# Gate features of block 2: the sigmoid from exponent and logarithm on ACT, in two halves a unit apart, in place of an exponential on ACT and a reciprocal on DVE

## The chip, the cores and the metric

The kernel runs as one program on one core of a Trainium2 chip. The metric is the device time of one execution in microseconds; the kernel is run several times and the median is taken. The profile is one more execution, recorded by the hardware profiler. The engines are named as the profile names them: PE is TensorE, PEld its weight loads, DVE VectorE, ACT ScalarE, POOL GpSimd, SP the queue that issues most DMAs.

## The reference, cut to what matters

Two blocks of two layers each, on 256 tokens of 1024 features. Block 2 has 256 more tokens, the context, beside them in its first layer. What the change touches is how block 2 gates the outputs of its two mixers. The gates' inputs are columns of one projection `p = h @ w_in`:

```python
# layer 0 of block 2 (512 rows: tokens and context)
aq, ak, av, hu, ag, hg = split_cols(p, EVEN_SPLITS)      # ag, hg: 512 columns each
y = concatenate([y_a * silu(ag), y_b * silu(hg)])        # global attention, Hyena branch
# layer 1 of block 2 (256 rows)
wq, wk, wv, nq, nk, nv, wg, ng = split_cols(p, ODD_SPLITS)
y = concatenate([y_w * silu(wg), y_n * silu(ng)])        # window, neighbourhood attention
x = x + gate * (y @ w_out)
```

`silu(x)` is `x * sigmoid(x)`. The four matrices have 8 x 128 columns in each layer, so there are 16 groups of 128 gate features.

## The kernel before, in words

The five engines run five streams written out by hand in one Python function; semaphores order them, and every engine takes its instructions strictly in the order in which they are written. Weights are fp32. Each quarter of a slab (1024 columns per partition) is split in two parts for the matmuls: ACT copies it to the rounded `w_high` (L1278), then DVE subtracts to get `w_low` (L1650). A product is three matmuls (L582, L583, L584). There are four split buffers. A split is written into ACT's and DVE's streams by `splits.due(...)`: at that place every quarter is split whose buffer has by then been used up on PE.

Block 2's attention runs over units u = 0 to 31 (`attention2`). In layer 0 a unit is one head of one tile of 128 query rows, and PE makes the scores of two units at once (L980); the scores are 512 wide for the two token tiles and 256 wide for the two context tiles. In layer 1 the first 16 units are window attention (kind W, with one small ACT exponential more, for the sink) and the last 16 neighbourhood attention (kind N), each 512 wide, scores at L1002.

In iteration u PE issues: the scores of u; the transposes of the softmax of u-1 (L1013, `second`), which wait for ACT's exponential; then the filler, which is a few steps of the projection by features (`feature_groups`, L582 to L584); then the product with the values of u-2 (L1031). One group of 128 features is 8 steps. In layer 0 there are 4 steps per unit, so a group ends every second unit (always an odd one); in layer 1 there are 2, so a group ends every fourth. Layer 0 has 20 groups: 12 go to the Hyena branch, the last 8 are gate features, ended in units 19, 21, 23, 25, 27, 29, 31 and 32. All 8 groups of layer 1 are gate features, ended in units 3, 7, ..., 31. A group is collected in one of the three PSUM banks 5 to 7; attention uses banks 0 to 4.

ACT in iteration u: copy of the transposed softmax of u-1 out of PSUM (L1285); exponential of the scores of u (L1513 in layer 0, L1314 in layer 1), which waits for DVE's maximum; `take_features` for the group that ended in u (L1494); the split that has come due; scaled copy of the output of u-2 (L1526).

DVE in iteration u: the split that has come due (`w_low` waits for ACT's `w_high`); mask and maximum of the scores of u (L2068, or L2075 and L2076), and the bias that ACT's exponential waits for; the reciprocal of the sum of u-1 (L2057, one column); `take_features` for the group that ended in u-1, which for gate features is `silu_finish`: add 1 (L2025), reciprocal (L2027), product with the feature itself (L2029). The last frees the bank.

Block 1 of the same kernel computes its own gates in the way that the change brings to block 2: |x| (L1383), exponential (L1390) and logarithm (L1392) on ACT, the exponent on DVE (L1782), the last exponential on ACT (L1398).

After the units of layer 0 DVE goes on with the hidden layers of the Hyena filter (L2150 on), then gates the attention output with `ag` (L2168). After those of layer 1 PE transposes the outputs (L1057), DVE gates them, and the last projection follows.

Of the kernel before, what the change touches and what calls it, by code (L numbers as in the profile page):

```python
# [211 lines left out]
def two_blocks(nc, A, C, out):  # L212
    ctx = ExitStack()
    with ctx:
# [250 lines left out]
        sin_ready = Signal(sem("sin_ready"), [(0,), (1,)])  # L465
        taps_guess = Signal(sem("taps_guess"), [(0,), (1,)])
        conv_begun = Signal(sem("conv_begun"), [(c,) for c in range(HY_CH)])
        silu_exp = Signal(sem("silu_exp"), [(l, c) for l in range(LAYERS) for c in range(8)])
        gates_of = [(l, n) for l in range(LAYERS) for n in range(6 * TILES)]
        gate_logged = Signal(sem("gate_logged"), gates_of)  # L470
        gates_ready = Signal(sem("gates_ready"), gates_of)
# [21 lines left out]
        def bank(*key):  # L493
            return banks[number[key][0]]
# [740 lines left out]
        def _(act):  # L1235
# [246 lines left out]
            def take_features(l, key):  # L1482

                c = key[2]
                splits.due(*key)
                if l == 0 and c < HY_CH:
                    act.wait_ge(*filled(*key))
                    run(A_(uc[:, c, :], bank(*key)[:, :], ACT.Identity, scale=conv_w[:, 1, c:c + 1], bias=conv_w[:, 3, c:c + 1]),
                        conv_begun.by(c))
                else:  # L1490
                    n, dst = (N4, (ag, hg)) if l == 0 else (SEQ, (wgT, ngT))
                    c -= HY_CH
                    act.wait_ge(*filled(*key))
                    run(A_(dst[c // 4][:, c % 4, :], bank(*key)[:, 0:n], ACT.Exp, scale=-1.0), silu_exp.by(l, c))  # L1494

            def attention2(l):
                U = units_of_block2(l)
                for u in range(len(U) + 2):
                    if 1 <= u <= len(U):
                        n = (2 if U[u - 1][0] == "G" and U[u - 1][2] >= TILES else 4) * P  # L1500
                        if u >= 3:
                            act.wait_ge(*filled("o", 2 + l, u - 3))
                        copy_out(PT[:, (u - 1) % 2, 0:n], bank("p", 2 + l, u - 1, 0)[:, 0:n], "p", 2 + l, u - 1, 0)
                    if u < len(U):
                        splits.due("s", 2 + l, u)
                        kind, h, t = U[u]
                        n = SEQ if kind == "G" and t >= TILES else N4
                        if kind == "G":

                            act.wait_ge(*bias_ready.at(2, u))  # L1510
                            if u >= 2:
                                act.wait_ge(*filled("p", 2 + l, u - 2, 0))
                            run(A_(S[:, u % 2, 0:n], bank("s", 2, u)[:, 0:n], ACT.Exp, bias=stat[:, u % 4, 1, 0:1],  # L1513
                                   scale=SCALE, accum_out=stat[:, u % 4, 2, 0:1]), emptied("s", 2, u))
                        else:
                            softmax_exp(2 + l, u, n, S[:, u % 2, 0:n], kind, SCALE)
                    for key in ended_in[(2 + l, u)]:
                        take_features(l, key)
                    if u >= 2:
                        kind, h, t = U[u - 2]  # L1520
                        dst = {"G": o2_tok, "W": o3_tok, "N": y3_tok}[kind]
                        key = ("o", 2 + l, u - 2)
                        splits.due(*key)
                        act.wait_ge(*filled(*key))
                        act.wait_ge(*sum_inverted.at(*key[1:]))
                        run(A_(dst[:, t, h * DH:(h + 1) * DH], bank(*key)[:, 0:DH], ACT.Copy, scale=stat[:, (u - 2) % 4, 2, 1:2]),  # L1526
                            emptied(*key))
# [88 lines left out]
        def _(dve):  # L1616
# [399 lines left out]
                    run(V.tensor_copy(small[:, 3:4], small[:, 3:4]), heads_ready.by(l, j))  # L2016
                run.settle()

            def silu_finish(l, key):

                c = key[2] - HY_CH
                n, dst = (N4, (ag, hg)) if l == 0 else (SEQ, (wgT, ngT))
                g = dst[c // 4][:, c % 4, :]
                dve.wait_ge(*silu_exp.at(l, c))
                run(V.tensor_scalar(g, g, 1.0, None, ALU.add))  # L2025
                run.settle()
                run(V.reciprocal(g, g))  # L2027
                run.settle()
                run(V.tensor_tensor(g, g, bank(*key)[:, 0:n], ALU.mult), emptied(*key))  # L2029

            def take_features(l, key):
                splits.due(*key)
                c = key[2]
                if l or c >= HY_CH:
                    return silu_finish(l, key)

                dve.wait_ge(*conv_begun.at(c))
                b = bank(*key)[:, :].rearrange("p (s n) -> p s n", s=2)
                u = uc[:, c, :].rearrange("p (s n) -> p s n", s=2)
                for s in range(2):  # L2040
                    run(V.scalar_tensor_tensor(out=u[:, s, 1:SEQ], in0=b[:, s, 0:SEQ - 1], scalar=conv_w[:, 0, c:c + 1],
                                               in1=u[:, s, 1:SEQ], op0=ALU.mult, op1=ALU.add))
                run.settle()
                for s in range(2):
                    run(V.scalar_tensor_tensor(out=u[:, s, 0:SEQ - 1], in0=b[:, s, 1:SEQ], scalar=conv_w[:, 2, c:c + 1],  # L2045
                                               in1=u[:, s, 0:SEQ - 1], op0=ALU.mult, op1=ALU.add), emptied(*key) if s else None)

            def attention2(l):
                U = units_of_block2(l)

                def invert_sum(u):
                    st = stat[:, u % 4, :, :]
                    dve.wait_ge(*probs_at(2 + l, u))
                    if U[u][0] == "W":
                        run(V.tensor_tensor(st[:, 2, 0:1], st[:, 2, 0:1], st[:, 3, 1:2], ALU.add))
                        run.settle()
                    run(V.reciprocal(st[:, 2, 1:2], st[:, 2, 0:1]), sum_inverted.by(2 + l, u))  # L2057

                for u in range(len(U) + 1):
                    splits.due("s", 2 + l, min(u, len(U) - 1))  # L2060
                    if u < len(U):
                        kind, h, t = U[u]
                        st = stat[:, u % 4, :, :]
                        n = SEQ if kind == "G" and t >= TILES else N4
                        b = bank("s", 2 + l, u)
                        dve.wait_ge(*filled("s", 2 + l, u))
                        if kind == "G":
                            run(V.tensor_reduce(st[:, 0, 0:1], b[:, 0:n], AX_X, ALU.max))  # L2068
                            run.settle()
                            run(V.tensor_scalar(st[:, 1, 0:1], st[:, 0, 0:1], -SCALE, None, ALU.mult), bias_ready.by(2 + l, u))  # L2070
                        else:
                            if u >= 2:
                                dve.wait_ge(*filled("p", 2 + l, u - 2, 0))
                            m = mask_w[:, t, :] if kind == "W" else rel_bias[:, t, h, :]
                            run(V.tensor_tensor_reduce(S[:, u % 2, 0:SEQ], b[:, 0:SEQ], m, 1.0, -3e38, ALU.add, ALU.max, st[:, 0, 0:1]))  # L2075
                            run(V.tensor_tensor_reduce(S[:, u % 2, SEQ:N4], b[:, SEQ:N4], no_mask, 1.0, -3e38, ALU.add, ALU.max,  # L2076
                                                       st[:, 0, 1:2]), emptied("s", 2 + l, u))
                            run.settle()
                            run(V.tensor_tensor(st[:, 0, 0:1], st[:, 0, 0:1], st[:, 0, 1:2], ALU.max))
                            run.settle()  # L2080
                            if kind == "W":

                                run(V.scalar_tensor_tensor(out=st[:, 1, 0:1], in0=st[:, 0, 0:1], scalar=-SCALE, in1=sink_neg[:, h:h + 1],
                                                           op0=ALU.mult, op1=ALU.min), bias_ready.by(2 + l, u))
                            else:
                                run(V.tensor_scalar(st[:, 1, 0:1], st[:, 0, 0:1], -SCALE, None, ALU.mult), bias_ready.by(2 + l, u))
                    if u >= 1:
                        invert_sum(u - 1)
                        for key in ended_in[(2 + l, u - 1)]:
                            take_features(l, key)  # L2090
                for key in ended_in[(2 + l, len(U))]:
                    take_features(l, key)

            def add_gated(l, n, columns, tiles, gate_b):
                for c in columns:
# [376 lines left out]
```

## Time and profile before

| what | value |
|---|---|
| median of 3 executions | 1634.72 us |
| the three | 1629.84, 1634.72, 7097.55 us |
| profiled execution, its time | 1633.1 us |
| profiled execution, its span | 1631.3 us |
| PE busy | 1543.8 us (95%) |
| DVE busy | 972.4 us (60%) |
| ACT busy | 778.4 us (48%) |
| mean granted TensorE clock | 0.977 |
| one matmul of 128x512 (L583), mean | 391 ns |

The span goes from the first to the last instruction; 1.8 us of the profiled execution's time lie around it. The busy shares are means over all stages. The units of block 2's layer 0 lie between 1064 and 1212 us from the start of the span, those with gate features from 1145 on; the units of layer 1 lie between 1481 and 1596 us.

### The profile page before, as it was taken

The numbers are of one execution on the slowest core, as the hardware profiler recorded it, in microseconds if no ns is written. First come the engines' busy times: TensorE is split into PE (matmuls) and PEld (weight loads), VectorE is DVE, ScalarE is ACT, GpSimd is POOL, SyncE is SP. The second block draws the span as 40 slices with busy tenths as digits, with TensorE's granted clock in tenths as the row PEclk, the third lists the DMA queues.
The fourth block names the chain that finished last, engine by engine and source line by source line (L and its number), as shares of the span: only waits on it lengthen the run. The fifth ranks groups of instructions, "written<-read, shape, count | busy, mean of one in ns | idle before, by whom it ended". The sixth has DMA issues, their size and how long they took to land.

```text
span 1631.3 us, 21300 instructions
## 1 busy us (share of the span) xinstructions
PE 1543.8 (95%) x8160; PEld 1236.0 (76%) x8160; DVE 972.4 (60%) x1757; ACT 778.4 (48%) x1321; POOL 63.4 (4%) x129
## 2 busy tenths in 40 slices
PE   6999999999999999999999999899968999999997
PEld 5887777799887888777899887778753477876675
DVE  4454457666445454457666556855786755685664
ACT  4546775455344446775455443345440013335652
POOL 4040000000000000000000000000000000400000
PEclk9999999999999999999999999999987999999999
DMA  8783335696555752434796553522220001542100
GB/s 252 241 181 101 111 106 198 191 274 182 198 186 191 250 180 79 129 104 155 228 258 188 191 177 125 140 78 57 73 78 13 0 27 52 137 146 62 52 1 26
DMA packets 183012, 220.94 MB, mean 135 GB/s; under 512 B 6507, under 2 KB 103317, under 8 KB 182848
## 3 DMA queue, kind: packets, MB, share of 16 engines
q1 hardware_dynamic: 179840, 211.65, 41.6%
q0 software_dynamic: 3072, 7.93, 2.5%
q8 instruction: 66, 1.08, 0.3%
q14 instruction: 34, 0.28, 0.1%
HBM read 216.55 MB, written 3.01 MB: 135 GB/s over the span
## 4 chain that ended last, share of the span: by engine, by line
PE 73%; DVE 16%; ACT 7%; issue 3%; DMA 1%; SPq 0%; ACTq 0%; DVEq 0%
PE bank L582 20%; PE bank L584 19%; PE bank L583 19%; DVE w_low L1650 2%; DVE arena L2027 2%; ACT w_high L1278 2%; PE bank L803 1%; PE bank L1013 1%; PE bank L1031 1%; PE bank L663 1%; PE bank L747 1%; PE bank L778 1%; PE bank L599 1%; PE bank L1136 1%; PE bank L1002 1%
## 5 line engine op out<-in xcount | busy, mean ns | idle before, releaser
L1650 DVE TENSOR_TENSOR w_low<-raw,w_high 128x1024 fp32r<-128x1024 f32 x352 | 425.2, 1214 | 405.8 <-ACT w_high L1278 400.2
L1278 ACT ACTIVATE w_high<-raw 128x1024 fp32r<-128x1024 f32 x352 | 366.7, 1046 | 369.3 <-PE bank L584 308.2
L582 PE MATMUL bank<-w_high,acts_r 128*128 128x512 f32 (+1 forms) x848 | 341.5, 403 | 20.8 <-DVE acts_r L1667 6.5
L584 PE MATMUL bank<-w_high,acts_r 128*128 128x512 f32 (+1 forms) x848 | 332.6, 392 | 0.0
L583 PE MATMUL bank<-w_low,acts_r 128*128 128x512 f32 (+1 forms) x848 | 331.8, 391 | 0.0
L582 PE MATMUL bank<-acts_r,w_high 128*128 128x256 f32 (+1 forms) x736 | 233.0, 317 | 2.2 <-DVE arena L2045 1.3
L584 PE MATMUL bank<-acts_r,w_low 128*128 128x256 f32 (+1 forms) x736 | 227.3, 309 | 0.0
L583 PE MATMUL bank<-acts_r,w_high 128*128 128x256 f32 (+1 forms) x736 | 227.0, 308 | 0.0
L582 PEld LDWEIGHTS bank<-w_high,acts_r 128*128 128x128 f32 x848 | 161.8, 191 | 63.3 <-DVE w_low L1650 12.9
L584 PEld LDWEIGHTS bank<-w_high,acts_r 128*128 128x128 f32 x848 | 160.8, 190 | 36.9
L583 PEld LDWEIGHTS bank<-w_low,acts_r 128*128 128x128 f32 x848 | 161.5, 190 | 32.6
L582 PEld LDWEIGHTS bank<-acts_r,w_high 128*128 128x128 f32 x736 | 140.2, 190 | 11.5 <-issue 3.5
L584 PEld LDWEIGHTS bank<-acts_r,w_low 128*128 128x128 f32 x736 | 139.2, 189 | 7.4
L583 PEld LDWEIGHTS bank<-acts_r,w_high 128*128 128x128 f32 x736 | 139.9, 190 | 6.0
L582 PE MATMUL bank<-w_high,hidden_r 128*128 128x512 f32 (+1 forms) x304 | 118.9, 391 | 0.0
L583 PE MATMUL bank<-w_low,hidden_r 128*128 128x512 f32 (+1 forms) x304 | 118.6, 390 | 0.0
L584 PE MATMUL bank<-w_high,hidden_r 128*128 128x512 f32 (+1 forms) x304 | 118.6, 390 | 0.0
L1285 ACT ACTIVATE arena<-bank 128x512 f32<-128x512 f32 (+3 forms) x168 | 83.4, 510 | 60.5 <-PE bank L1013 28.2
L584 PEld LDWEIGHTS bank<-w_high,hidden_r 128*128 128x128 f32 x304 | 57.3, 188 | 13.2
L583 PEld LDWEIGHTS bank<-w_low,hidden_r 128*128 128x128 f32 x304 | 57.3, 188 | 13.0
L582 PEld LDWEIGHTS bank<-w_high,hidden_r 128*128 128x128 f32 x304 | 57.3, 188 | 13.0
L1031 PEld LDWEIGHTS bank<-arena 128*128 128x128 f32 x448 | 57.6, 191 | 3.2 <-ACT arena L1285 0.5
(298 smaller groups left out, 1790.5 us busy)
## 6 DMA issues: line engine op xcount, KB each, us to landing
raw<-in_w_in SPq DMA_DIRECT2D x70, 1024.0 KB, 5.2
raw<-in_w_up SPq DMA_DIRECT2D x64, 512.0 KB, 6.8
raw<-in_w_down SPq DMA_DIRECT2D x32, 1024.0 KB, 5.0
raw<-in_w_ada SPq DMA_DIRECT2D x24, 1024.0 KB, 7.5
raw<-in_w_in SPq DMA_DIRECT2D x32, 512.0 KB, 4.6
raw<-in_w_o SPq DMA_DIRECT2D x8, 1024.0 KB, 7.4
raw<-in_w_out SPq DMA_DIRECT2D x8, 1024.0 KB, 5.1
raw<-in_w_out_c SPq DMA_DIRECT2D x4, 768.0 KB, 5.3
```

What stands on the lines that cost most here:

```text
L582: mm(o, lh, rh, start=start, stop=False)
L583: mm(o, lh, rl, start=False, stop=False)
L584: return mm(o, ll, rh, start=False, stop=stop)
L599: ins = mm(o[:, c:c + P], X[:, x0 + t, k * P:(k + 1) * P], scales[:, t, 0:P], start=True, stop=True)
L663: ins = mm(o[32 * j:32 * (j + 1), :], cond[:, 4 * h + j, :], w[:, j, :], start=h == 0, stop=h == 1)
L747: ins = mm(o[:, c:c + span], head(0, hd, q), head(1, hd, slice(0, span)), start=True, stop=True)
L778: ins = tr(o[:, (b - b0) * P:(b - b0 + 1) * P], S[:, u % 2, b * P:(b + 1) * P], ident[:, :])
L1031: ins = mm(o[:, 0:DH], PT[:, u % 2, n * P:(n + 1) * P], v, start=n == 0, stop=n == len(blocks) - 1)
L1278: run(A_(high, src, ACT.Copy), (high_ready, n + 1))
L1285: run(A_(dst, src, ACT.Copy, scale=scale), emptied(*key))
L1650: run(V.tensor_tensor(low, src, high.bitcast(F32), ALU.subtract), (split_ready, n + 1))
L2027: run(V.reciprocal(g, g))
```

## The change: what it does

The sigmoid of a feature x was 1 / (1 + exp(-x)). It becomes exp(min(x, 0) - ln(1 + exp(-|x|))), which is the same value. Per group of gate features:

- ACT, in the iteration in which it took exp(-x): |x|, then exp(-|x|), then ln(1 + that), each waiting for the one before; then it signals `silu_logged`.
- DVE, where it had `silu_finish`: one instruction, min(x, 0) minus the logarithm; it signals `silu_exponent`.
- ACT, one iteration later, right behind that unit's softmax exponential: `finish_silu`, which waits for the exponent and takes its exponential; it signals `silu_exp`.
- DVE, one iteration after its exponent: `finish_silu`, the product with x out of PSUM, which frees the bank.

DVE's add and reciprocal are gone. On ACT the group has four activations where it had one. PE, POOL and SP keep their streams.

```diff
@@ semaphores
-        silu_exp = Signal(sem("silu_exp"), [(l, c) for l in range(LAYERS) for c in range(8)])
+        silu_of = [(l, c) for l in range(LAYERS) for c in range(8)]
+        silu_logged = Signal(sem("silu_logged"), silu_of)
+        silu_exponent = Signal(sem("silu_exponent"), silu_of)
+        silu_exp = Signal(sem("silu_exp"), silu_of)
@@ ACT, take_features
-                    run(A_(dst[c // 4][:, c % 4, :], bank(*key)[:, 0:n], ACT.Exp, scale=-1.0), silu_exp.by(l, c))
+                    x = dst[c // 4][:, c % 4, :]
+                    run(A_(x, bank(*key)[:, 0:n], ACT.Abs))
+                    run.settle()
+                    run(A_(x, x, ACT.Exp, scale=-1.0))
+                    run.settle()
+                    run(A_(x, x, ACT.Ln, bias=eps_col[:, 1:2]), silu_logged.by(l, c))
+                    begun.append((l, c, x))
+
+            begun = []
+
+            def finish_silu():
+
+                while begun:
+                    l, c, x = begun.pop(0)
+                    act.wait_ge(*silu_exponent.at(l, c))
+                    run(A_(x, x, ACT.Exp), silu_exp.by(l, c))
@@ ACT, attention2, between the softmax exponential and take_features
+                    finish_silu()
                     for key in ended_in[(2 + l, u)]:
                         take_features(l, key)
@@ DVE
-            def silu_finish(l, key):
+            begun = []
+
+            def silu_exponent_of(l, key):
 
                 c = key[2] - HY_CH
                 n, dst = (N4, (ag, hg)) if l == 0 else (SEQ, (wgT, ngT))
                 g = dst[c // 4][:, c % 4, :]
-                dve.wait_ge(*silu_exp.at(l, c))
-                run(V.tensor_scalar(g, g, 1.0, None, ALU.add))
-                run.settle()
-                run(V.reciprocal(g, g))
-                run.settle()
-                run(V.tensor_tensor(g, g, bank(*key)[:, 0:n], ALU.mult), emptied(*key))
+                dve.wait_ge(*silu_logged.at(l, c))
+                run(V.scalar_tensor_tensor(out=g, in0=bank(*key)[:, 0:n], scalar=0.0, in1=g, op0=ALU.min, op1=ALU.subtract),
+                    silu_exponent.by(l, c))
+                begun.append((l, c, g, key, n))
+
+            def finish_silu():
+
+                while begun:
+                    l, c, g, key, n = begun.pop(0)
+                    dve.wait_ge(*silu_exp.at(l, c))
+                    run(V.tensor_tensor(g, g, bank(*key)[:, 0:n], ALU.mult), emptied(*key))
@@ DVE, take_features
-                    return silu_finish(l, key)
+                    return silu_exponent_of(l, key)
@@ DVE, attention2
                         invert_sum(u - 1)
+                        finish_silu()
                         for key in ended_in[(2 + l, u - 1)]:
                             take_features(l, key)
+                finish_silu()
                 for key in ended_in[(2 + l, len(U))]:
                     take_features(l, key)
+                finish_silu()
```

## Rows read from the trace of the kernel before

**Rows 1.** Page, part 4: the chain that ended last, shares of the span by line.
```profile
PE bank L582 20%; PE bank L584 19%; PE bank L583 19%; DVE w_low L1650 2%; DVE arena L2027 2%; ACT w_high L1278 2%; PE bank L803 1%; PE bank L1013 1%; PE bank L1031 1%; PE bank L663 1%; PE bank L747 1%; PE bank L778 1%; PE bank L599 1%; PE bank L1136 1%; PE bank L1002 1%
```

**Rows 2.** Groups by line and shape, 1140 to 1600 us: busy, mean ns | idle before.
```profile
L1013 PE MATMUL bank<-ident,arena 128*128 128x128 f32 x168 | 29.0, 293 | 7.5 <-ACT arena L1314 5.9 <-ACT arena L1513 1.3
L2027 DVE RECIPROCAL arena<-arena 128x512 f32<-128x512 f32 x8 | 26.8, 3354 | 0.3
L2027 DVE RECIPROCAL arena<-arena 128x256 f32<-128x256 f32 x8 | 14.0, 1753 | 0.3
```

**Rows 3.** Waits, 1140 to 1212 us: who waited for whom, total, times, longest.
```profile
PE bank L980 <- ACT arena L1513: 2.6, 3, 1.2
```

**Rows 4.** Busy time in the stretch of layer 1's gate groups: PE, PEld, DVE, ACT.
```profile
1496.00:1592.00 96.00, 90.94 (x566) 66.77 (x566) 58.73 (x238) 56.28 (x142) 0.00 (x0) 1.00 0.07 23
```

**Rows 5.** Timeline of PE, layer 1, kind W: start, duration, operation [idle before].
```profile
1497.43 0.66 PE L1013 MATMUL bank<-ident,arena 128*128 128x128 f32 x4
...
1501.18 0.66 PE L1013 MATMUL bank<-ident,arena 128*128 128x128 f32 x4 [0.49 <-ACT arena L1314]
...
1504.96 0.66 PE L1013 MATMUL bank<-ident,arena 128*128 128x128 f32 x4 [0.52 <-ACT arena L1314]
...
1508.15 0.66 PE L1013 MATMUL bank<-ident,arena 128*128 128x128 f32 x4
```

**Rows 6.** Timeline of ACT, the same stretch.
```profile
1496.45 0.36 ACT L1494 ACTIVATE arena<-bank 128x256 f32<-128x256 f32 x1
1496.72 1.04 ACT L1278 ACTIVATE w_high<-raw 128x1024 fp32r<-128x1024 f32 x1
...
1500.33 0.71 ACT L1314 ACTIVATE arena<-arena,stat 128x512 f32<-128x512 f32 x1
```

**Rows 7.** Timeline of PE, layer 1, kind N.
```profile
1552.88 0.66 PE L1013 MATMUL bank<-ident,arena 128*128 128x128 f32 x4
...
1556.25 0.65 PE L1013 MATMUL bank<-ident,arena 128*128 128x128 f32 x4
...
1559.82 0.66 PE L1013 MATMUL bank<-ident,arena 128*128 128x128 f32 x4 [0.31 <-ACT arena L1314]
```

**Rows 8.** All of block 1's such activations, by line and shape.
```profile
L1392 ACT ACTIVATE arena<-arena,eps_col 128x512 f32<-128x512 f32 x24 | 17.4, 724 | 0.8
...
L1390 ACT ACTIVATE arena<-arena 128x512 f32<-128x512 f32 x24 | 15.1, 629 | 0.0
```

**Rows 9.** Timeline of ACT, layer 0, end of the gate groups.
```profile
1206.20 0.60 ACT L1494 ACTIVATE arena<-bank 128x512 f32<-128x512 f32 x1 [4.28 <-PE bank L584]
1206.69 1.05 ACT L1278 ACTIVATE w_high<-raw 128x1024 fp32r<-128x1024 f32 x1
```

**Rows 10.** Timeline of PE, layer 0, between two gate groups' ends and the next transposes.
```profile
1145.16 1.00 PE L1031 MATMUL bank<-arena 128*128 128x64 f32 x8
...
1150.77 0.39 PE L1013 MATMUL bank<-ident,arena 128*128 128x128 f32 x2
...
1153.80 1.00 PE L1031 MATMUL bank<-arena 128*128 128x64 f32 x8
...
1158.73 0.39 PE L1013 MATMUL bank<-ident,arena 128*128 128x128 f32 x2
```

**Rows 11.** Timeline of ACT, layer 0: the split behind a gate group, the next softmax.
```profile
1154.69 1.06 ACT L1278 ACTIVATE w_high<-raw 128x1024 fp32r<-128x1024 f32 x1
...
1157.56 0.47 ACT L1513 ACTIVATE arena<-bank,stat 128x256 f32<-128x256 f32 x1 [1.34 <-DVE stat L2070]
...
1163.53 1.06 ACT L1278 ACTIVATE w_high<-raw 128x1024 fp32r<-128x1024 f32 x1
...
1166.67 0.69 ACT L1513 ACTIVATE arena<-bank,stat 128x512 f32<-128x512 f32 x1 [1.45 <-DVE stat L2070]
```

**Rows 12.** Timeline of DVE, end of layer 0's gate groups.
```profile
1210.68 0.69 DVE L2029 TENSOR_TENSOR arena<-arena,bank 128x512 f32<-128x512 f32 x1
```

**Rows 13.** Groups by line on ACT, whole span: one of three table loads.
```profile
L1549 ACT ACT_TABLE_LOAD x1 | 1.3, 1283 | 0.0
```

## The prediction

> **What bounds the kernel now.** I read the page first, then the chain of waits, then the two stretches in which the changed code runs, with PE's idle time and the timelines of three engines. The chain is PE for the most part; the reciprocal L2027 holds 2% of it, as much as a whole side of the weight split [rows 1]. That share tempts: the two widths of the reciprocal make 26.8 + 14.0 = 40.8 us of DVE time [rows 2], 2.5% of the span, and nearly all of it is replaced by 16 short instructions. But the chain goes through DVE there only because DVE and PE are nearly level. The reader should ask what PE would do if the reciprocals were gone. PE is busy 90.9 of 96 us in layer 1's stretch [rows 4], so at most about 5 us are to be had there. In all of it the transposes L1013 waited 5.9 us for the softmax of layer 1 and 1.3 us for that of layer 0 [rows 2], and the scores L980 waited 2.6 us for a bank that the softmax had not yet freed [rows 3]. So layer 0 has 1.3 + 2.6 = 3.9 us of stall, layer 1 about 6, and not 41 us.
>
> **Which wait ends last in layer 1.** There a gate group ends every four units. Four starts of L1013 give three distances: 3.75, 3.78 and 3.19 us [rows 5]. The last is PE's own pace; the fourth distance of the period is the same. So each period has two stalls, 0.56 and 0.59 us. They have different causes. The first comes before any reciprocal: ACT took its exponential at 1496.45 and began w_high at 1496.72; DVE can subtract only after that, and only then masks the next unit's scores; the softmax began at 1500.33 and PE went on at 1501.18 [rows 5, 6]. The second stall is the reciprocal's: it stands on DVE between two units' masks. In kind N the distances are 3.37 and 3.57 us [rows 7], stalls of 0.18 and 0.38 us. The change takes away the second stall and makes the first longer, since three dependent activations now stand on ACT ahead of w_high.
>
> **What the longer ACT part costs.** Block 1's rows give 0.63 us for the exponential and 0.72 us for the logarithm at 512 columns, and 0.8 us of idle over 24 logarithms, 0.03 us for each dependent start [rows 8]. |x| reads PSUM as the old exponential did and I price it the same, 0.60 us at 512 [rows 9] and 0.36 us at 256 columns [rows 6]; the difference, 0.24 us, also takes exponential and logarithm at 256 to 0.39 and 0.48 us, an estimate from these rows. At 256 columns w_high then starts 0.36 + 0.03 + 0.39 + 0.03 + 0.48 - 0.09 (overlap with the next) = 1.20 us after |x|, where it started 0.27 us after [rows 6]: 0.93 us later. At 512 columns it is 0.60 + 0.03 + 0.63 + 0.03 + 0.72 - 0.11 = 1.90 us, against 0.49 us [rows 9]: 1.41 us later. Bounds of this delay: 0, if PE has slack for all of it, and these sums plus the fourth activation (0.39 or 0.63 us), if the last exponential also falls on the path. I take the sums, since no slack is left where PE stalls already.
>
> **Layer 1.** Kind W, per period: first stall 0.56 + 0.93 = 1.49 us, second 0, against 1.15 us: +0.34, three times. Kind N: 0.18 + 0.93 = 1.11 us against 0.56: +0.55, three times. The period that goes from W to N I put between, +0.45. Sum 1.02 + 1.65 + 0.45 = 3.1 us. The eighth group ends in unit 31 and has ACT's copy of the last softmax behind it, and PE's last product with the values waits for that copy; it moves by 0.93 us. Layer 1: **+4.0 us**.
>
> **Layer 0.** There a group ends every two units. Its last matmul is issued just ahead of L1031 and takes 0.39 us (table above), so I put its end 0.2 us, half of that, behind the start of L1031. From there PE needs, without waiting, 1150.77 - 1145.36 = 5.4 us until the transposes that need the next softmax, or 1158.73 - 1154.00 = 4.7 us, by the widths of the units [rows 10]; six groups count, three of each, the order by the unit order being 5.4, 4.7, 4.7, 5.4, 5.4, 4.7. The chain to be fitted in after the change is 1.90 us to w_high, then 1157.56 - 1154.69 = 2.87 us to the softmax at 256 columns (3.14 us at 512, from 1163.53 to 1166.67) [rows 11], then the softmax until PE can start: 0.85 us at 512 columns [rows 5, 6] and 0.47 + 0.14 = 0.61 us at 256. That is 5.38 us at 256 and 5.89 us at 512 (the third and fourth groups, ahead of token tiles). Against the intervals, in that order: 0, 0.65, 1.16, 0.48, 0, 0.65 us, together 2.9 us of new stalls. The 3.9 us of old ones go: they came from the 3.35 us of reciprocal [rows 2] on DVE between two maxima. Net -1.0 us. After the last group, DVE's product (which the Hyena layers stand behind) began at 1210.68, 4.48 us after ACT took the group [rows 9, 12]. After the change: 2.01 us for the three activations; w_high (already issued behind them) until 2.96; the copy of an output until 3.2; the exponential until 3.83, DVE's exponent (0.69) being done beside w_high. So 0.65 us sooner. Layer 0: **-1.65 us**.
>
> **Costed at nothing.** DVE's exponent and product, 0.69 us each at 512 columns by the row of the old product [rows 12]: they are covered by the 40.8 us taken from DVE. ACT's last exponential: it stands behind the softmax and ahead of two copies, for the second of which ACT waits on PE's transposes anyway; without that cover it is 8 x 0.63 + 8 x 0.39 = 8.2 us. Its wait on DVE: DVE has the exponent within some 0.8 us of the bias that releases the softmax (0.69 us), about when ACT is there. The bank, freed a unit later: there are three and the next use is two groups on. The split, later by 0.93 or 1.41 us: four buffers, its next use is three groups on. SP's loads follow the splits by as much, with DMA at a 0.07 share there [rows 4]. POOL's stream has nothing of it.
>
> **Sum.** +4.0 - 1.65 = +2.35 us on the profiled execution's own 1633.1 us (span 1631.3): **1635.5 us**. That execution lies 1.6 us under the median of the runs shown, 1634.72, and 3.3 us over their lowest, 1629.84; what runs differ by is more than what I forecast.
>
> **Rivals.**
> 1. *ACT's three activations are hidden* and only the reciprocal's stalls go. Layer 1 gets back 3 x 0.59 + 3 x 0.38 + 0.49 = 3.4 us, layer 0 3.9 + 0.65 us, together 8.0: 1625 us. For it: ACT is busy 56 of 96 us in layer 1 [rows 4]. Against: the first stall of each period is already there, behind ACT's shorter part [rows 5]. Chance 0.18.
> 2. *The last exponential is on the path*: ACT waits in it for an exponent that is queued on DVE behind w_low and the masks, and the copies that PE waits for come late. 2.35 + 8.2: 1644 us. For it: two engines hand over in both directions within one unit. Against: the order puts the softmax before it, and DVE is then nearly idle. Chance 0.08.
> 3. *Slower by over 2%: the activation tables are switched* between exponential and logarithm. Each group would load two, 16 x 2 x 1.28 = 41 us [rows 13], all ahead of w_high or on ACT's copies: 1633.1 + 41 = 1674 us. It decides as soon as one load per group appears. Against: 24 exponentials and logarithms alternate in block 1 with no load between them [rows 8], only three loads stand in the span, and the one at L1549 belongs to the sine. Chance 0.03.
>
> The Trainium skill, page "ScalarE activation tables: per-element evaluation and per-set limits", section "Table sets in the compiler and the runtime", says that the back end places the loads per block by the longest run; that could put a switch in here, and the trace so far has none. By "ScalarE: Activation LUTs", section "What ACT_TABLE_LOAD costs", a switch is about 2.66 us with its drain, which would make rival 3 an estimated 85 us; the load's own 1283 ns is what the trace shows too.
>
> 4. *The gain that the chain's share promises*, 33 us or more: 1600 us. It needs PE to run without its own work; PE's pace of 3.19 us per unit forbids it. Chance 0.01.
>
> **How the numbers follow.** The forecast has 0.70. The range reaches from near rival 1, with the spread of runs, to rival 2: 1626 to 1643 us, which leaves out a part of each and rivals 3 and 4. Two per cent is about what a measurement here can tell from no change; that is 32.7 us, and only rivals 4 and 3 pass it. Faster 0.01, within 2% 0.96, slower 0.03.
>
> **What would show it.** DVE busy falls by the 40.8 us of reciprocals, with 16 exponents for 16 shorter additions against it, so by 35 to 40 us; ACT busy rises by some 8 x 1.98 + 8 x 1.26 = 26 us. In layer 1 the distances of L1013 become about 4.7 (W) and 4.3 us (N) once in four units and 3.19 us otherwise; L1013 waits longer in sum than now while L980 waits no more. w_high begins 1.2 and 1.9 us after |x|. The forecast is wrong if the distances after a group stay under 4 us (rival 1), if a second one in the period stays above 3.4 us (rival 2), or if a table load stands among the units (rival 3).

## The result: 0.9% slower, and outside the stated range

| | before | after |
|---|---|---|
| median | 1631.35 us (5 executions) | 1647.47 us (5 executions, 1640.41 to 1649.29) |
| ratio of after to before | | 1.0088, 95% interval 1.0061 to 1.0115 |
| profiled execution: span | 1631.3 us | 1647.3 us |
| PE / DVE / ACT busy | 1543.8 / 972.4 / 778.4 us | 1556.3 / 933.7 / 801.4 us |
| mean granted TensorE clock | 0.977 | 0.973 |

The median of before counts one slow execution of 7097.55 us; the ratios compare fast executions alone. The forecast was 1635.5 us in a range from 1626 to 1643 us. The change is slower by 14 us (by the ratio) to 16 us (by the medians and the profiled executions) where 2.35 us were forecast. DVE lost 38.7 us of work (forecast 35 to 40) and ACT got 23.0 us more (forecast 26). No table load was added: the trace of after has three, as before.

**The profile after.** Groups by line and shape between 1140 and 1612 us of the changed kernel, for the transposes that wait for the softmax and the parts of the new silu:

```profile
L1016 PE MATMUL bank<-ident,arena 128*128 128x128 f32 x168 | 30.6, 305 | 12.6 <-ACT arena L1317 10.1 <-ACT arena L1531 2.4
...
L1502 ACT ACTIVATE arena<-arena,eps_col 128x256 f32<-128x256 f32 x8 | 4.1, 509 | 0.3
L1500 ACT ACTIVATE arena<-arena 128x256 f32<-128x256 f32 x8 | 3.3, 416 | 0.3
L2046 DVE SCALAR_TENSOR_TENSOR arena<-bank,arena 128x256 f32<-128x256 f32 x8 | 3.3, 407 | 1.1 <-ACT arena L1502 1.1
```

L1016 (L1013 before) now idles 12.6 us where it idled 7.5 [rows 2]: 10.1 us in layer 1 against 5.9. But the same 168 transposes also took 305 ns each and not 293. That second number is where the surprise begins.

The timeline of ACT behind the first gate group of layer 1, after:

```profile
1491.98 0.36 ACT L1498 ACTIVATE arena<-bank 128x256 f32<-128x256 f32 x1
1492.38 0.42 ACT L1500 ACTIVATE arena<-arena 128x256 f32<-128x256 f32 x1
1492.82 0.51 ACT L1502 ACTIVATE arena<-arena,eps_col 128x256 f32<-128x256 f32 x1
1493.24 1.04 ACT L1281 ACTIVATE w_high<-raw 128x1024 fp32r<-128x1024 f32 x1
```

w_high starts 1.26 us after |x|; it started 0.27 us after the old exponential [rows 6]. The sum of the prediction had 1.20 us. And PE's starts of L1016 in layer 1, after, kind W:

```profile
1507.28 0.66 PE L1016 MATMUL bank<-ident,arena 128*128 128x128 f32 x4
1512.02 0.66 PE L1016 MATMUL bank<-ident,arena 128*128 128x128 f32 x4 [1.48 <-ACT arena L1317]
1515.21 0.66 PE L1016 MATMUL bank<-ident,arena 128*128 128x128 f32 x4
1518.41 0.66 PE L1016 MATMUL bank<-ident,arena 128*128 128x128 f32 x4
1521.60 0.66 PE L1016 MATMUL bank<-ident,arena 128*128 128x128 f32 x4
1526.34 0.66 PE L1016 MATMUL bank<-ident,arena 128*128 128x128 f32 x4 [1.48 <-ACT arena L1317]
...
1531.40 1.11 PE L1016 MATMUL bank<-ident,arena 128*128 128x128 f32 x4
```

These answer to [rows 5]. Up to 1526 all is as forecast: one distance of 4.74 us per period (forecast 4.7), three of 3.19 or 3.20 us, the second stall gone. Then 1526.34 to 1531.40, 5.06 us, has no wait in it at all: the four transposes took 1.11 us where they take 0.66. The same instructions take 1.7 times as long. The busy times and the clock of stretches say why. After, one stretch of 2 us inside the 5.06 us and four of 20 us:

```profile
1528.00:1530.00 2.00, 2.00 (x8) 1.77 (x8) 0.00 (x0) 0.89 (x3) 0.00 (x0) 0.50 0.00 0
...
1500.00:1520.00 20.00, 18.52 (x116) 13.57 (x117) 9.67 (x51) 12.39 (x34) 0.00 (x0) 1.00 0.16 52
1520.00:1540.00 20.00, 18.52 (x96) 13.53 (x96) 7.00 (x35) 11.94 (x32) 0.00 (x0) 0.83 0.00 1
...
1560.00:1580.00 20.00, 18.21 (x95) 14.04 (x95) 7.89 (x40) 11.16 (x28) 0.00 (x0) 0.79 0.00 1
1580.00:1600.00 20.00, 18.90 (x87) 13.19 (x87) 6.32 (x31) 9.04 (x22) 0.00 (x0) 0.76 0.00 1
```

(columns: stretch, length, busy time and count of PE, PEld, DVE, ACT and POOL, granted clock, DMA share, GB/s). PE is busy 18.5 us in each of the first two of 20 us, but with 116 instructions and then with 96. Before, the clock was 1.00 in this part [rows 4]. The granted clock has two levels, 2.4 GHz (1.00) and 1.2 GHz (0.50, as from 1528 to 1530 us); a stretch of 20 us at 0.8 is one in which PE spent some of its time at either. PE's busy share hides this: it does not fall between the first two. The clock falls in this way behind the third to the seventh gate group of layer 1, each time for some microseconds.

**Where the 16.0 us of span went**, by marks in both traces. From the transposes of the first softmax behind a gate group in layer 1 to those of the last unit: 1497.70 to 1606.53, 108.8 us, after; 1501.18 to 1591.83, 90.65 us, before; +18.2 us. The end, from there to the last instruction: 40.8 against 39.5 us, +1.3 us. Everything ahead of the first of these marks: -3.5 us. In the latter is an accident of the clock the other way, 3.0 us: the kernel before had its first two distances of layer 1 at 4.33 and 4.25 us (1485.66, 1489.99, 1494.24), with the clock at 0.78 from 1480 to 1490 us, and the changed kernel, with its clock at 1.00 there, had them at 2.35 and 3.20 us. The first longer stall, which lies ahead of the mark, takes 1.0 us of that back (4.74 for 3.75 us); the rest, 1.4 us, lies ahead of layer 1.

### The profile page after: what moved, and what is told of

Same layout as the page of the kernel before. It is cut to its first block, busy times and chain, and to the rows that moved or that the text cites. A ratio compares the mean times of both kernels' runs of the same rounds, so it can differ in the third digit from the quotient of the medians.

```text
span 1647.3 us, 21332 instructions
## 1 busy us (share of the span) xinstructions
PE 1556.3 (94%) x8160; PEld 1246.9 (76%) x8160; DVE 933.7 (57%) x1741; ACT 801.4 (49%) x1369; POOL 63.4 (4%) x129
## 4 chain that ended last, share of the span: by engine, by line
PE 77%; DVE 12%; ACT 7%; issue 2%; DMA 1%; SPq 0%; ACTq 0%; DVEq 0%
PE bank L585 20%; PE bank L587 20%; PE bank L586 20%; DVE w_low L1669 2%; PE bank L1034 2%; ACT w_high L1281 2%; PE bank L1016 2%; PE bank L1005 1%; PE bank L806 1%; PE bank L750 1%; PE bank L666 1%; PE bank L781 1%; PE bank L602 1%; PE bank L1139 1%; ACT arena L1317 1%
## 5 line engine op out<-in xcount | busy, mean ns | idle before, releaser
L1034 PEld LDWEIGHTS bank<-arena 128*128 128x128 f32 x448 | 63.7, 210 | 4.2 <-ACT arena L1288 1.5
```

The source lines that it names most:

```text
L1034: ins = mm(o[:, 0:DH], PT[:, u % 2, n * P:(n + 1) * P], v, start=n == 0, stop=n == len(blocks) - 1)
```

## The experiments

Ten kernels, each timed against the kernel before on the same chip as itself. Three theories stood after the comparison. **Clock**: the longer stall, once in four units, makes the granted clock fall in layer 1, and that is 12 us or more of the loss. **Hand-overs**: the two crossings between ACT and DVE and the fourth activation cost. **Both layers alike**: the two-part silu is dearer everywhere.

### Each layer alone

```diff
-        silu_logged = Signal(sem("silu_logged"), silu_of)
+        silu_logged = Signal(sem("silu_logged"), [(L, c) for c in range(8)])   # L: the layer with the change
...
+                    if l == 1 - L:       # ACT, and likewise DVE: as in the kernel before
+                        run(A_(x, bank(*key)[:, 0:n], ACT.Exp, scale=-1.0), silu_exp.by(l, c))
+                        return
```

Layer 0 alone. 

> The change in layer 0 alone; layer 1 keeps exponential, addition and reciprocal. Theory (the loss is layer 1's: there PE stands still longer once in four units and the granted clock falls): layer 0's own balance was -1.65 us by the prediction and about -1.9 us in the traces (offset between the two kernels' marks at the first gate group and at the last product of layer 0), so 1 to 3 us under the kernel before, clock in layer 1 as before. Rival (the two-part silu costs in both layers): slower than before by half of the 14 us, about 7 us.

Measured: 1627.99 us, ratio 0.9973 (0.9964 to 0.9983), which is 4 us less. Its times alone are used here, not its trace, so its clock in layer 1 was not read; the mean clocks of its timed executions, 0.980 to 0.984, are like those of the kernel before. The two-part silu makes layer 0 faster, as the prediction said; the size is over this expectation by 1 us and over the prediction's term by 2.4 us.

Layer 1 alone. 

> The change in layer 1 alone. Theory: all of the loss and a little more, 1645 to 1650 us, with L1013's distance after a group 4.7 and 4.3 us and the granted clock near 0.8 from the third or fourth gate group on. Rival (both layers): about 1638 us.

Measured: 1654.0 us, ratio 1.0133 (1.0115 to 1.0152). The whole loss is layer 1's, and somewhat more than the change as a whole, 4 us over the top of the expectation. In its trace the clock fell at the first gate group already (1498.72, transposes of 1.11 us) and came back, and it was not low throughout. The third theory is out.

### PE kept at work in the stall

```diff
-                    pe.wait_ge(*probs_at(2 + l, u))
                     o = open_bank("p", 2 + l, u, 0, among=ATTENTION_BANKS)
+                    if l == 1 and u and u % 4 == 0:
+                        for _ in range(10 if u < 16 else 7):
+                            tr(o[:, 0:P], ident[:, :], ident[:, :])
+                    pe.wait_ge(*probs_at(2 + l, u))
```

> The changed kernel, and on PE in layer 1, in the place where it waits for the softmax behind a gate group, 10 (kind W) or 7 (kind N) more 128x128 transposes of the identity into the bank that the real ones then overwrite: 10 x 0.147 = 1.5 us and 1.0 us, as long as the stalls. PE does more work, and nothing that it waits for comes sooner. Theory (12 of the 16 us that layer 1 lost are the clock, which falls when PE stands still in the stall): the clock stays at 2.4 GHz through layer 1, the long distances stay at 4.4 to 4.9 us, the others are 3.19 us, and the time is that of the prediction's sum, some 2 to 4 us over the kernel before: 1633 to 1637 us. Rival 1 (the clock falls for another reason, such as the total of work or the fewer DVE instructions): 1647 us as the changed kernel. Rival 2 (the distances after the first stalls grew by waits, not by the clock): 1647 us or more.

Measured: 1633.65 us (1632.98 to 1638.1), ratio 1.0013 (1.0004 to 1.0022). PE does 58 transposes more (3 x 10 and 4 x 7) and the kernel is 12 us (by the ratios) to 14 us (by the medians) faster than the change without them. The timeline of PE at the third gate group, where the changed kernel lost its clock (L1016 are the added transposes, L1019 the real ones):

```profile
1525.73 1.31 PE L1016 MATMUL bank<-ident 128*128 128x128 f32 x10
1527.28 0.66 PE L1019 MATMUL bank<-ident,arena 128*128 128x128 f32 x4 [0.23 <-ACT arena L1320]
1530.47 0.66 PE L1019 MATMUL bank<-ident,arena 128*128 128x128 f32 x4
```

and the stretches of 20 us:

```profile
1500.00:1520.00 20.00, 19.77 (x127) 14.58 (x126) 8.87 (x46) 12.49 (x34) 0.00 (x0) 1.00 0.15 54
1520.00:1540.00 20.00, 19.77 (x127) 14.63 (x125) 9.57 (x45) 13.87 (x35) 0.00 (x0) 1.00 0.00 1
...
1560.00:1580.00 20.00, 19.82 (x126) 14.63 (x126) 7.48 (x38) 13.29 (x32) 0.00 (x0) 1.00 0.00 1
```

The real transposes of 1527.28 come 4.74 us after their predecessors, as in the changed kernel: the wait for ACT is exactly as long. What follows is 3.19 us, at 1.00. Between the marks used above this kernel takes 1498.64 to 1591.86, 93.2 us: between them the longer stalls cost 93.2 - 90.65 = 2.6 us net of those removed, and the clock costs 108.8 - 93.2 = 15.6 us. The first longer stall lies ahead of the first mark; with its 1.0 us the net cost of the seven periods is 3.6 us (forecast 3.1).

The same transposes two units away from the stall (`u % 4 == 2`), where PE does not wait. 

> The changed kernel with the same 10 or 7 extra transposes on PE per period of layer 1, two units away from the stall, where PE does not wait. Theory (the clock is kept by filling the stall itself): the stalls stay, the clock falls, and the extra work costs 7 x 1.2 = 8 us on top: 1650 to 1660 us. Rival (more work on PE anywhere in the period keeps the clock): 1634 + 8 = 1642 us, clock full.

Measured: 1652.86 us, ratio 1.0138 (1.0116 to 1.0159); its stretches from 1500 to 1560 us were at 0.81, 0.85 and 0.83. As much work put at this other place in the period does not keep the clock; put into the stall it does. This answers the rival that the total of PE's work decides.

### The kernel before, made slow on ACT alone

```diff
-                    run(A_(dst[c // 4][:, c % 4, :], bank(*key)[:, 0:n], ACT.Exp, scale=-1.0), silu_exp.by(l, c))
+                    x = dst[c // 4][:, c % 4, :]
+                    run(A_(x, bank(*key)[:, 0:n], ACT.Exp, scale=-1.0), None if l else silu_exp.by(l, c))
+                    for m in range(copies if l else 0):
+                        run.settle()
+                        run(A_(x, x, ACT.Copy), silu_exp.by(l, c) if m == copies - 1 else None)
```

One copy. 

> The kernel before (exponential, addition, reciprocal, product), with one 128x256 copy of the gate features onto themselves on ACT behind the exponential, in layer 1 alone: about 0.42 us more ahead of w_high once in four units. Theory (what stands ahead of w_high makes PE's first stall longer, one for one, and from some length on the granted clock falls in layer 1): stalls alone give 7 x 0.42 + 0.4 = 3.4 us over the kernel before, 1635 us; with the clock already falling, up to 1645 us. Rival (the loss of the changed kernel comes from its hand-overs between ACT and DVE, which this kernel has not): 1632 to 1635 us and the clock full.

Measured: 1636.71 us, ratio 1.0034 (1.0023 to 1.0046). PE's starts of L1013 in this kernel, and two stretches:

```profile
1515.21 0.91 PE L1013 MATMUL bank<-ident,arena 128*128 128x128 f32 x4 [0.94 <-ACT arena L1314]
1519.98 0.66 PE L1013 MATMUL bank<-ident,arena 128*128 128x128 f32 x4
...
1530.56 0.66 PE L1013 MATMUL bank<-ident,arena 128*128 128x128 f32 x4 [0.93 <-ACT arena L1314]
1534.34 0.66 PE L1013 MATMUL bank<-ident,arena 128*128 128x128 f32 x4 [0.52 <-ACT arena L1314]
1537.53 0.66 PE L1013 MATMUL bank<-ident,arena 128*128 128x128 f32 x4
```

```profile
1500.00:1520.00 20.00, 17.70 (x101) 13.39 (x101) 12.37 (x48) 11.58 (x32) 0.00 (x0) 0.91 0.16 54
1520.00:1540.00 20.00, 18.55 (x120) 14.19 (x120) 11.40 (x52) 12.18 (x33) 0.00 (x0) 1.00 0.00 1
```

The first stall grew by 0.44 us, one for one, and the reciprocal's stayed. From 1520 to 1600 us the clock was at 1.00. Behind the second gate group it fell once, though: after the wait of 0.94 us the transposes took 0.91 us, and the next distance was 4.77 us where the others of its kind are 3.77 to 3.78. The time, 4.5 us more, is the sum of the stalls, 3.5 us, and about 1.0 us of this. One copy alone does not decide between the theories, since both had a time near it.

Two copies. 

> As the one with one copy, with two copies: about 0.84 us more ahead of w_high, near the 0.93 us of the change, and DVE keeps its reciprocals. Theory: stalls alone 6.7 us, and the clock falls as in the changed kernel or more, since the reciprocal's stall remains beside the longer one: 1645 to 1660 us. Rival (hand-overs): the stalls alone, 1638 us, clock full.

Measured: 1647.8 us, ratio 1.0099 (1.0073 to 1.0125), the same as the change. No hand-over was added, no reciprocal taken away, so the second theory is not needed for a loss of this size; the kernel with the short part on ACT, below, puts it out. PE's starts behind its first gate group, and two stretches:

```profile
1501.48 0.66 PE L1013 MATMUL bank<-ident,arena 128*128 128x128 f32 x4 [1.39 <-ACT arena L1314]
1506.92 1.11 PE L1013 MATMUL bank<-ident,arena 128*128 128x128 f32 x4
1512.85 1.11 PE L1013 MATMUL bank<-ident,arena 128*128 128x128 f32 x4
```

```profile
1500.00:1520.00 20.00, 18.61 (x80) 14.16 (x80) 9.06 (x40) 9.13 (x24) 0.00 (x0) 0.66 0.01 2
...
1560.00:1580.00 20.00, 17.79 (x108) 12.63 (x107) 11.04 (x42) 12.38 (x31) 0.00 (x0) 1.00 0.01 1
1580.00:1600.00 20.00, 19.66 (x85) 14.70 (x86) 8.69 (x33) 8.80 (x22) 0.00 (x0) 0.66 0.00 0
```

With a wait of 1.39 us the clock falls at some of the groups and comes back; with 0.93 us it fell once, briefly, and held from 1520 us on. One copy more (0.42 us, 7 or 8 times) costs 11 us more. Which of the groups it falls at differs: here the first, in the changed kernel the third.

### The silu of the change with a short part on ACT

The exponential and the logarithm between |x| and the exponent are left out, so the gates are not the reference's:

```diff
                     run(A_(x, bank(*key)[:, 0:n], ACT.Abs))
-                    run.settle()
-                    run(A_(x, x, ACT.Exp, scale=-1.0))
-                    run.settle()
-                    run(A_(x, x, ACT.Ln, bias=eps_col[:, 1:2]), silu_logged.by(l, c))
```

(the signal `silu_logged` moves to |x|.) 

> The changed kernel with the exponential and the logarithm between |x| and DVE's exponent left out in both layers (the gates are then not the reference's); |x|, the exponent on DVE, the last exponential and the product stay, so ACT has as much ahead of w_high as the kernel before, and both hand-overs remain. Theory (only the three activations' length ahead of w_high costs): what the prediction's first rival gave, 8 us under the kernel before, 1624 us, clock full. Rival (the hand-overs and the last exponential cost): 1632 us or more.

Measured: 1622.25 us, ratio 0.9936 (0.9921 to 0.9951): 10 us less. Both hand-overs and the last exponential are in it and cost nothing that can be seen. Behind a gate group of kind W:

```profile
1508.11 0.66 PE L1016 MATMUL bank<-ident,arena 128*128 128x128 f32 x4 [0.49 <-ACT arena L1317]
1511.31 0.66 PE L1016 MATMUL bank<-ident,arena 128*128 128x128 f32 x4
```

The first stall is the old one to the hundredth [rows 5], and the second is gone. What the additions and reciprocals cost is real, up to 10 us; it is what stood in their place on ACT that took more.

### w_high first

```diff
+                    splits.due(*key, ahead=1)
                     act.wait_ge(*filled(*key))
                     x = dst[c // 4][:, c % 4, :]
                     run(A_(x, bank(*key)[:, 0:n], ACT.Abs))
```

> The changed kernel with the order of two things on ACT exchanged: when a gate group has ended, w_high of the quarter that it frees comes first and the three activations behind it. Theory (the three activations cost by standing ahead of w_high, w_low, the masks and the next softmax): the first stall of a period in layer 1 shrinks to 0.56 - 0.27 = 0.29 us (W) and 0 (N), the second is gone with the reciprocal; layer 0 has no stalls. Layer 1 -5 us, its end +0.9 us, layer 0 -3.9 us, its end 0: 8 us under the kernel before, about 1623 us, clock at its full level. Rival (the fourth activation or the two hand-overs are what costs, wherever the three stand): no faster than the changed kernel by more than its stalls, 1640 us or more.

Measured: 1622.96 us (1622.09 to 1623.42), ratio 0.9946 (0.9932 to 0.9959), 9 us under the kernel before and 24 under the change, by one line. ACT and PE in this kernel, kind W:

```profile
1500.60 1.04 ACT L1281 ACTIVATE w_high<-raw 128x1024 fp32r<-128x1024 f32 x1
1501.54 0.36 ACT L1499 ACTIVATE arena<-bank 128x256 f32<-128x256 f32 x1
1501.94 0.42 ACT L1501 ACTIVATE arena<-arena 128x256 f32<-128x256 f32 x1
```

```profile
1505.06 0.66 PE L1016 MATMUL bank<-ident,arena 128*128 128x128 f32 x4 [0.22 <-ACT arena L1317]
1508.25 0.66 PE L1016 MATMUL bank<-ident,arena 128*128 128x128 f32 x4
```

The stall is 0.22 to 0.29 us (1505.06 less the start before, 1501.58, less 3.19), as expected, and the clock is 1.00 from 1480 to 1580 us.

The exchange of order without the new silu. 

> The kernel before, with its reciprocals, and only the exchange of order on ACT: w_high ahead of the exponential of a gate group. Theory: w_high and all behind it come 0.27 us (layer 1) sooner, the first stall of a period shrinks by that or to nothing, the reciprocal's stall stays: 3 x 0.27 + 4 x 0.2 = 1.6 us, layer 0 nothing (there the reciprocal sets the stall), so 1 to 2 us under the kernel before, about 1630.5 us. Rival (the exchange alone is what made the faster kernel fast): 8 us less, 1623 us.

Measured: 1625.32 us (1622.76 to 1628.48), ratio 0.9964 (0.995 to 0.9977): 6 us less, where 1 to 2 were expected. In its trace the second stall of a W period is there, unchanged (0.51 us); in kind N only one distance in four is longer than 3.20 us, 3.46 to 3.48 us. Between the marks layer 1 takes 1.7 us less, as expected. The expectation missed two things. In layer 0 the reciprocals, too, come behind w_low, so they also begin sooner: from the second pair of scores to the last it took 119.6 us against 121.3 before. And its profiled execution had the clock at 1.00 from 1480 to 1490 us, where the one before had 0.78; that is 3 us (its first two distances are 2.35 and 3.19 us) which I cannot assign to the edit from single traces. So the exchange alone is worth 6 of the 9 us of the kernel with w_high first and both changes, and the rival, that it is all of it, was nearer than I had allowed. The intervals of the two ratios, 0.9932 to 0.9959 and 0.995 to 0.9977, overlap: that the new silu gains anything beyond the exchange, 2 to 3 us by the medians, is not clear of the noise.

The last gate group of layer 1 behind ACT's copies:

```diff
+                    late = l == 1 and u >= len(U) - 1     # then finish_silu and take_features of u-1 come last
```

> The changed kernel with w_high first, and in layer 1 the last gate group, ended in unit 31, is taken on ACT behind the copies of that unit's softmax and of the output of unit 30, and finished behind the last output's copy. Theory (the three activations there stand ahead of the copies that PE's last product waits for): 0.9 to 1.2 us less than with w_high first alone, less up to 0.6 us if DVE's product then comes late for the gating: 1621.5 to 1622.5 us. Rival (DVE's product is then what the gating waits for, by more than is won): no change or slower, 1623 to 1625 us.

Measured: 1620.76 us (1618.37 to 1623.58), ratio 0.9927 (0.9914 to 0.9941). It has the lowest median of the study, 11 us under the kernel before. Its lead of 2 us over the kernel with w_high first alone lies within its own spread of 5 us and is not shown.

| kernel | median, us | ratio to before | interval |
|---|---|---|---|
| changed kernel | 1647.47 | 1.0088 | 1.0061 to 1.0115 |
| layer 0 alone | 1627.99 | 0.9973 | 0.9964 to 0.9983 |
| layer 1 alone | 1654.0 | 1.0133 | 1.0115 to 1.0152 |
| work in the stall | 1633.65 | 1.0013 | 1.0004 to 1.0022 |
| work elsewhere | 1652.86 | 1.0138 | 1.0116 to 1.0159 |
| before, one copy | 1636.71 | 1.0034 | 1.0023 to 1.0046 |
| before, two copies | 1647.8 | 1.0099 | 1.0073 to 1.0125 |
| exponential, logarithm left out | 1622.25 | 0.9936 | 0.9921 to 0.9951 |
| w_high first | 1622.96 | 0.9946 | 0.9932 to 0.9959 |
| before, w_high first | 1625.32 | 0.9964 | 0.995 to 0.9977 |
| w_high first, last group late | 1620.76 | 0.9927 | 0.9914 to 0.9941 |

## Why the prediction was wrong, point by point

- **What bounds, and the ceiling.** Right. The 40.8 us of reciprocals were worth 10 us at the most (the kernel with the short ACT part, which keeps the rest), near the 8 us of the rival with 1625 us. The 9 us of w_high first are not a second measure of it, since the exchange of order alone gave 6 of them.
- **The two stalls and their causes.** Right: the one behind w_high grew, the one behind the reciprocal went, in every kernel by its own cause.
- **The price on ACT.** 1.20 us forecast, 1.26 measured at 256 columns; 1.90 forecast, 1.92 measured at 512. The distances 4.7 and 4.3 us came out as 4.74 and 4.36.
- **Layer 1, +4.0 us.** This is the step that failed. Its stalls were nearly right (3.1 us forecast, 3.6 measured in the kernel with the filled stall). The end, 0.93 us forecast, measured 1.3 us in the changed kernel and 1.9 us in the one with the filled stall. But the sum priced a wait of PE at its own length, and the instructions behind it at the full clock, because every row of layer 1 from which it was made was at 1.00 [rows 4]. I never asked whether the clock would survive a stall three times as long. It did not: 15.6 us between the marks, four times the term. The trace before showed that it could happen: the one wait of the transposes in layer 1 that was longer than 1 us, 1.11 us at 1485.66, was followed by transposes of 1.12 us, and the clock was 0.78 from 1480 to 1490 us. The changed kernel has the same wait, 1.11 us at 1484.22, and kept its clock at 1.00 there.
- **Layer 0, -1.65 us.** Right in sign, about 1.9 by the traces, 4 us by the times of the kernel with layer 0 alone. The four stalls of 0.65, 1.16, 0.48 and 0.65 us were 0.49, 1.06, 0.41 and 0.48 us, and DVE's last product came 0.97 us sooner by the clock of the trace. Its clock held, at 1.00 from 1080 to 1200 us, through a new wait of 1.06 us; in this layer PE has twice the filler per unit, but that this is the reason is not shown.
- **Costed at nothing.** Right for the last exponential, the bank, the split buffers and the loads: the kernel with the short part on ACT has all of them and is faster by 10 us, where 8 us were expected of it.
- **Rivals.** None held what happened. The one with the last exponential on the path had the nearest time (1644 us) by a wrong cause. No table was switched. The fifth one, missing, was: the stall that is moved to one place is long enough for the granted clock to fall.

What stays open: at which of the groups the clock falls, and why the first units of layer 1 find it low in some executions. The executions of the changed kernel go from 1640 us at a mean clock of 0.975 to 1649 us at 0.973, the others with 0.970 and 0.971, so the loss itself varies by several microseconds. The length of the single wait does not decide alone. In the changed kernel 1.48 us at the first two groups left the clock at 1.00, while 1.10 us in kind N was followed by a fall three times out of three:

```profile
1560.69 0.66 PE L1016 MATMUL bank<-ident,arena 128*128 128x128 f32 x4 [1.10 <-ACT arena L1317]
1565.91 1.11 PE L1016 MATMUL bank<-ident,arena 128*128 128x128 f32 x4
```

With two copies on ACT, one wait of 1.00 us was followed by a fall and another was not; with one copy, one of three waits of 0.93 or 0.94 us was. What the runs show is that falls became more frequent as the wait behind a gate group grew, and that work in this wait prevented them.

## What to carry to other kernels

A wait of PE can cost more than its own length. When a change makes one longer, ask what the granted clock does, for the instructions behind a fall can cost more than the wait, here 15.6 against 3.6 us, and PE's busy share does not show it. Whether one long stall is worse than two of the same sum was not separated. In kind N the changed kernel waited 1.10 us in one piece per period and lost the clock three times out of three, while the kernel before with two copies waited 1.00 us and 0.31 us in two pieces in one such period and kept it, and lost it behind 1.00 us in the next. In kind W, 1.48 us in one piece (changed kernel) and 0.93 + 0.52 us in two (one copy) each lost it in one period of three. Count instructions per stretch beside busy time. When work is moved onto an in-order engine, look at what is queued behind it first; here the split that DVE, the masks and the next softmax hang on only had to be put ahead of it, by one line, for the loss of 16 us to become a gain of 9, most of which this order gives to the old silu too.

## What the runs showed of the hardware that was not expected

The granted clock fell to its lower level again and again in a stage in which PE was busy 91% to 95% of each stretch of 20 us (1520 to 1600 us of the changed kernel) and never waited longer than 1.48 us at once; its transposes then took 1.11 us for 0.66. Ten transposes of the identity (seven in kind N), 1.3 us of work with no use, put into that wait, kept it at its upper level through the stage (1.00 from 1500 to 1580 us) and made the kernel 12 to 14 us faster; the same ones two units away from the wait did not (0.81 to 0.85 from 1500 to 1560 us).
